# A hybrid decoder block's forget gate: the tokens become the stationary side of its small matmuls, and two transposes go

## The chip, the cores and the metric

The kernel runs on one core of a Trainium2 chip. The metric is the device time of one launch in microseconds (us); lower is better. Three runs of the kernel before took 1178.87, 1178.98 and 1179.95 us (median 1178.98 us).

## The reference, cut to what matters

The layer is one block of a decoder: 256 tokens of width 2048, three attention branches, gates, and an output projection. Everything is float32. One input projection of the normed tokens feeds the branches; eight of its columns are the forget gate's logits `fb`, one for each head of branch B.

```
h = _rmsnorm(x, norm_g[l])
proj = h @ w_in[l]
qa, ka, va, za, qb, kb, vb, zb, fb, qm, zm, gl = _split_cols(proj, IN_WIDTHS)   # fb: 8 columns
...
log_f = jax.nn.log_sigmoid(fb.astype(jnp.float32) + b_forget[l].astype(jnp.float32))
ob = _forgetting_attention(qb, kb, vb, log_f)    # logit[t,s] += sum of log_f over s < j <= t
```

So the gate needs, for each of 256 tokens, 8 sums over 2048 products. It is a very small part of the work: the other columns of `w_in` are 18,432 in number.

## The kernel before, in words

All matmuls on large operands use a split of each float32 value into a high part (the rounded value in the matmul's own 32-bit format, fp32r) and a low part (the rest). A product is then three matmuls: high by high, high tokens by low weights, low tokens by high weights. `hT` holds the high and low parts of the normed tokens, transposed: 128 partitions of the width's rows by 16 tiles `k` by 256 tokens. `mT` is the same for the memory tokens. ScalarE makes the high part of each weight tile (`hi`), VectorE the low part (`lo`), and TensorE runs the three matmuls (`passes`, lines 1220 to 1222) with the tokens as the stationary side and 512 weight columns moving.

The work is cut into units `s` of two weight tiles. A unit is 12 matmuls. Each engine has its own instruction stream in the order in which the code is written, and semaphores tie them together; nothing reorders the streams. In the first 32 units (`body("m", 0, None)`) each engine also runs `beside_first(s)` ahead of or behind unit `s`; this is where tokens and memory tokens are transposed and where the forget gate is computed.

The forget gate's steps before the change, all in the first body:

- TensorE, ahead of unit 12 (lines 1353 to 1362): for each of 16 tiles `k` two matmuls, with the gate's weights as the stationary side (16 columns: the high and low parts of 8 gate columns; then the 8 high ones) and 256 tokens moving. They add up in the PSUM bank `side[0]`, 16 partitions by 256 tokens. The weights lie in a part of the tile `ozT_hi` that is free then (`wf_both`, `wf_hi`).
- VectorE, behind unit 14 (lines 1016 to 1018): a copy of the 16 x 256 result into SBUF (`fbT`, a part of the tile `group`).
- TensorE, ahead of unit 15 (lines 1369 to 1375): two transposes of it, 16 x 128 to 128 x 16, into `side[1]`; then a wait for `dvec_sb`, which has nothing to do with the gate.
- VectorE, behind unit 16 (from line 1021): the sums of the two parts, scaling, bias, and the start of the log sigmoid; ScalarE and VectorE finish it in units 17 to 20, and TensorE forms the running sums over tokens ahead of unit 22 (lines 1380 to 1385).

Ahead of unit 12 TensorE waits for `mT_lo` (the last low part of the memory tokens, VectorE, line 1012) and for the gate's low weights. The tokens' parts `hT` have been there for several units.

Of the kernel before, what the change touches and what calls it, by code (L numbers as in the profile page):

```python
# [37 lines left out]
P = 128  # L38
D = 2048
S = 256  # L40
TT = S // P
KT = D // P
CW = 512
A_HEADS, B_HEADS, M_HEADS, HD, MD = 12, 8, 4, 128, 256
# [68 lines left out]
def hybrid_block(nc, x, mem, norm_g, mem_norm_g, w_in, b_forget, b_gate, rel_bias,  # L113
# [4 lines left out]
    def sb(name, shape, dt=F32):  # L118
        return nc.alloc_sbuf_tensor(name, shape, dt)

    hT = [sb("hT_hi", [P, KT, S], F32R), sb("hT_lo", [P, KT, S], F32R)]
# [8 lines left out]
    def part(at, n):  # L130
        return group[:, at:at + n]
# [22 lines left out]
                                          for at in (8, 12, 16, 20))  # L154
    mem_sb = part(0, 2 * D).rearrange("p (t c) -> p t c", t=TT)
    waste = part(3 * D, D)
    fbT = part(5120, S)[0:2 * B_HEADS]
    cT = part(5120, S)[0:B_HEADS]

    gates = [part(at, 1024).rearrange("p (t c) -> p t c", t=TT) for at in (4096, 1024, 2048)]  # L160
# [7 lines left out]
    ident = cst[:, 0:P]  # L168
# [10 lines left out]
    wf_both = ozT[0][:, 0, 0:KT * 2 * B_HEADS].rearrange("p (k h) -> p k h", k=KT)  # L179
    wf_hi, wf_lo = wf_both[:, :, 0:B_HEADS], wf_both[:, :, B_HEADS:]  # L180
    bf = sb("bf", [P, B_HEADS])
    ls = [sb(f"ls{i}", [P, TT, B_HEADS]) for i in range(8)]
    ccol = sb("ccol", [P, TT, B_HEADS])
# [26 lines left out]
    side = [nc.alloc_psum_tensor(f"side{i}", [P, CW], F32) for i in range(4)]  # L210
# [3 lines left out]
    def x_bank(k):  # L214
# [30 lines left out]
    pre = {n: sem("pre_" + n) for n in (  # L245
        "half rel gains gxT gx sumx0 sumx1 sumx meanx rootx halfx xT x_hi x_lo wf_hi wf_lo dvec dvec_sb dvec_out w_hi w_lo "
        "summ meanm rootm mTp mT_hi mT_lo "
        "fbT fbT_sb fb vb v0 v1 vneg e u ln log1p lf ccol ccol_sb crow_sb crow_out crow_in0 crow_in1 fbias").split()}


    x_v = x.rearrange("b (t p) d -> (b p) t d", p=P)
# [24 lines left out]
    with block as block:  # L276
# [500 lines left out]
        def _(dve):  # L777
# [13 lines left out]
            def chain(name, n, ins):  # L791
                ins.then_inc(pre[name], 1)
                dve.wait_ge(pre[name], n)
# [182 lines left out]
            def beside_first(s):  # L976
# [29 lines left out]
                for r in range(2):  # L1006
                    for j in range(4):
                        if s == 8 + 3 * r + j // 2:
                            dve.wait_ge(pre["mT_hi"], 4 * r + j + 1)
                            for i in range(2):  # L1010
                                k = 8 * r + 2 * j + i
                                o = dve.scalar_tensor_tensor(mT[1][:, k], side[j][:, i * S:(i + 1) * S],
                                                             gm[:, k:k + 1], mT[0][:, k].bitcast(F32),
                                                             ALU.mult, ALU.subtract)
                            o.then_inc(pre["mT_lo"], 1)
                if s == 14:
                    dve.wait_ge(pre["fbT"], 1)
                    dve.tensor_copy(fbT, side[0][0:2 * B_HEADS, 0:S]).then_inc(pre["fbT_sb"], 1)
                if s == 16:

                    dve.wait_ge(pre["fb"], 1)
                    both = side[1][:, 0:TT * 2 * B_HEADS].rearrange("p (t w h) -> p t w h", t=TT, w=2)
                    for t in range(TT):
                        o = dve.scalar_tensor_tensor(ls[1][:, t], both[:, t, 1], rsx[:, t:t + 1], bf[:],
                                                     ALU.mult, ALU.add)
                    chain("vb", 1, o)
                    for t in range(TT):
                        o = dve.scalar_tensor_tensor(ls[0][:, t], both[:, t, 0], rsx[:, t:t + 1], ls[1][:, t],
                                                     ALU.mult, ALU.add)
                    chain("v0", 1, o)  # L1030
                    chain("v1", 1, dve.tensor_scalar(ls[1][:], ls[0][:], -1.0, None, ALU.mult))
                    dve.tensor_tensor(ls[2][:], ls[0][:], ls[1][:], ALU.min).then_inc(pre["vneg"], 1)
# [26 lines left out]
            def body(kind, g, attn, b=None):  # L1059
                u0 = g * BODY_U  # L1060
                for s in range(BODY_U):
# [9 lines left out]
                    if attn is None:  # L1071
                        beside_first(s)
                    else:
                        for t in range(TT):
                            if s == U_Z[t] + 1:
                                silu(attn[1], t)
                        attention(*attn, s)
# [31 lines left out]
            c0 = 4 * GROUPS  # L1109
# [105 lines left out]
        def _(pe):  # L1215
            def passes(s, x_pair, k, j, t, banks, first, last):

                tok = slice(t * P, (t + 1) * P)
                hi, lo = x_pair[0][:, k + j, tok], x_pair[1][:, k + j, tok]
                pe.matmul(banks[t][:], hi, whi[:, s % RING, j], start=first and j == 0, stop=False)  # L1220
                pe.matmul(banks[t][:], hi, wlo[:, s % RING, j], start=False, stop=False)  # L1221
                return pe.matmul(banks[t][:], lo, whi[:, s % RING, j], start=False, stop=last and j == UK - 1)  # L1222
# [86 lines left out]
            def tokens_T(b):  # L1309

                pe.wait_ge(x_in[b], 16)
                for j in range(X_COLS[b] // 256, X_COLS[b + 1] // 256):
                    if j >= 6:
                        pe.wait_ge(pre["x_lo"], 2 * (j - 5))
                    for i in range(2):
                        for t in range(TT):
                            k = 2 * j + i
                            o = pe.transpose(x_bank(k)[:, t * P:t * P + P], x_sb[:, t, k * P:(k + 1) * P], ident)  # L1318
                    o.then_inc(pre["xT"], 1)
# [18 lines left out]
            def beside_first(s):  # L1338
                if s in U_X:
                    tokens_T(U_X.index(s))  # L1340
                if s in (7, 10):
                    r = (7, 10).index(s)
                    pe.wait_ge(mem_in[r], 16)

                    pe.wait_ge(*((pre["mT_lo"], 4) if r else (pre["x_lo"], KT)))
                    for k in range(8 * r, 8 * r + 8):
                        bank = side[(k % 8) // 2]
                        for t in range(TT):
                            c0 = (k % 2) * S + t * P
                            o = pe.transpose(bank[:, c0:c0 + P], mem_sb[:, t, k * P:(k + 1) * P], ident)  # L1350
                        if k % 2:
                            o.then_inc(pre["mTp"], 1)
                if s == 12:

                    pe.wait_ge(pre["mT_lo"], 8)
                    pe.wait_ge(pre["wf_lo"], 1)
                    for k in range(KT):
                        pe.matmul(side[0][0:2 * B_HEADS, 0:S], wf_both[:, k], hT[0][:, k], start=k == 0, stop=False,  # L1358
                                  skip_group_check=True)
                        o = pe.matmul(side[0][0:B_HEADS, 0:S], wf_hi[:, k], hT[1][:, k], start=False,  # L1360
                                      stop=k == KT - 1, skip_group_check=True)
                    o.then_inc(pre["fbT"], 1)
                if s == 13:

                    pe.wait_ge(small_in, 16 * 9)
                    pe.wait_ge(pre["rel"], 1)
                    pe.matmul(side[2][0:A_HEADS, 0:SEG], rel[:], oh[:], start=True, stop=True)\
                      .then_inc(pre["dvec"], 1)
                if s == 15:
                    pe.wait_ge(pre["fbT_sb"], 1)  # L1370
                    for t in range(TT):
                        o = pe.transpose(side[1][:, 2 * t * B_HEADS:2 * (t + 1) * B_HEADS],
                                         fbT[:, t * P:(t + 1) * P], ident[0:2 * B_HEADS, 0:2 * B_HEADS])
                    o.then_inc(pre["fb"], 1)
                    pe.wait_ge(pre["dvec_sb"], 1)
                if s == 22:
                    pe.wait_ge(cst_in, 16)

                    pe.wait_ge(pre["lf"], 1)
                    pe.matmul(side[0][:, 0:B_HEADS], tri[:, 0:P], ls[7][:, 0], start=True, stop=True)  # L1380
                    pe.matmul(side[0][:, B_HEADS:2 * B_HEADS], tri[:, P:S], ls[7][:, 0], start=True, stop=False)
                    pe.matmul(side[0][:, B_HEADS:2 * B_HEADS], tri[:, 0:P], ls[7][:, 1], start=False, stop=True)

                    pe.matmul(side[1][0:B_HEADS, 0:S], ls[7][:, 0], tri, start=True, stop=False)
                    pe.matmul(side[1][0:B_HEADS, P:S], ls[7][:, 1], tri[:, 0:P], start=False, stop=True)\
                      .then_inc(pre["ccol"], 1)
# [25 lines left out]
            c0 = 4 * GROUPS  # L1412
# [20 lines left out]
            for s in range(NCH * CU):  # L1433
# [12 lines left out]
                for t in range(TT):  # L1446
                    for j in range(UK):
                        o = passes(s, mT, UK * (s % CU), j, t, acc[(s // CU) % 2], False, True)
# [45 lines left out]
```

## Time and profile before

| what | value |
|---|---|
| median of three runs | 1178.98 us (1178.87 to 1179.95) |
| profiled execution | 1178.6 us, of which the span of instructions is 1176.8 us |
| TensorE matmuls busy | 1170.0 us, 99% of the span |
| TensorE weight loads busy | 971.9 us, 83% (they lie beside matmuls) |
| VectorE busy | 718.4 us, 61% |
| ScalarE busy | 537.8 us, 46% |
| DMA | 230 GB/s on average |

The span runs from the first to the last instruction of the profiled execution; the execution's own time is 1.8 us longer. A matmul's duration in the trace holds the time until its result is written, and matmuls overlap: with 512 columns moving one is shown as 0.39 us, and the next starts 0.23 us after it. What a matmul costs in a stream is therefore the distance between starts, not its duration. Weight loads (PEld) are rows of their own: "128*16" in a matmul's row is its stationary operand of 128 partitions by 16 columns, and the shape behind it is the moving one.

### The profile page before, as it was taken

The numbers are of one execution on the slowest core, as the hardware profiler recorded it, in microseconds if no ns is written. First come the engines' busy times: TensorE is split into PE (matmuls) and PEld (weight loads), VectorE is DVE, ScalarE is ACT, GpSimd is POOL, SyncE is SP. The second block draws the span as 40 slices with busy tenths as digits, with TensorE's granted clock in tenths as the row PEclk, the third lists the DMA queues.
The fourth block names the chain that finished last, engine by engine and source line by source line (L and its number), as shares of the span: only waits on it lengthen the run. The fifth ranks groups of instructions, "written<-read, shape, count | busy, mean of one in ns | idle before, by whom it ended". The sixth has DMA issues, their size and how long they took to land.

```text
span 1176.8 us, 14683 instructions
## 1 busy us (share of the span) xinstructions
PE 1170.0 (99%) x5332; PEld 971.9 (83%) x5332; DVE 718.4 (61%) x886; ACT 537.8 (46%) x660; POOL 40.6 (3%) x31
## 2 busy tenths in 40 slices
PE   8999999999999999999999999999999999999998
PEld 7888888888888888888888888888888888888887
DVE  5768576576576566567576565665556556555643
ACT  5755445444544544545544444434434443543332
POOL 1100000000010000000000000000000000000000
PEclk9999999999999999999999999999999999999999
DMA  9778678668678587687777786567549547765761
GB/s 312 258 242 309 222 229 295 193 201 312 195 248 282 181 266 260 209 263 225 252 236 237 252 259 216 170 223 254 200 147 302 184 161 225 249 210 204 249 226 38
DMA packets 143848, 270.54 MB, mean 230 GB/s; under 512 B 8833, under 2 KB 29493, under 8 KB 143808
## 3 DMA queue, kind: packets, MB, share of 16 engines
q1 hardware_dynamic: 132032, 253.33, 64.6%
q10 hardware_dynamic: 11488, 16.62, 4.5%
q8 instruction: 25, 0.41, 0.1%
q0 software_dynamic: 288, 0.06, 0.1%
q14 instruction: 15, 0.12, 0.0%
HBM read 248.72 MB, written 23.62 MB: 231 GB/s over the span
## 4 chain that ended last, share of the span: by engine, by line
PE 99%; DMA 0%; DVE 0%; issue 0%
PE acc L1220 32%; PE acc L1221 31%; PE acc L1222 31%; PE side L1270 1%; PE side L1266 0%; PE side L1286 0%; PE acc L1325 0%; PE side L1295 0%; PE side L1297 0%; PE side L1293 0%; PE side L1271 0%; PE side L1350 0%; PE side L1318 0%; DMA cst<-in_consts_dram 0%; PE side L1358 0%; PE side L1360 0%
## 5 line engine op out<-in xcount | busy, mean ns | idle before, releaser
L788 DVE TENSOR_TENSOR w_lo<-w_raw,w_hi 128x1024 fp32r<-128x1024 f32 x407 | 496.1, 1222 | 394.9 <-ACT w_hi L484 394.3
L484 ACT ACTIVATE w_hi<-w_raw 128x1024 fp32r<-128x1024 f32 x407 | 430.1, 1060 | 548.3 <-PE acc L1222 543.5
L1220 PE MATMUL acc<-w_hi,hT_hi 128*128 128x512 f32 x1152 | 450.1, 391 | 0.1
L1222 PE MATMUL acc<-w_hi,hT_lo 128*128 128x512 f32 x1152 | 448.5, 389 | 0.0
L1221 PE MATMUL acc<-w_lo,hT_hi 128*128 128x512 f32 x1152 | 448.4, 389 | 0.0
L1220 PEld LDWEIGHTS acc<-w_hi,hT_hi 128*128 128x128 f32 x1152 | 216.3, 188 | 45.9 <-DVE w_lo L788 1.3
L1222 PEld LDWEIGHTS acc<-w_hi,hT_lo 128*128 128x128 f32 x1152 | 216.2, 188 | 45.2
L1221 PEld LDWEIGHTS acc<-w_lo,hT_hi 128*128 128x128 f32 x1152 | 216.3, 188 | 44.0
L1220 PE MATMUL acc<-w_hi,mT_hi 128*128 128x512 f32 x256 | 100.4, 392 | 0.0
L1222 PE MATMUL acc<-w_hi,mT_lo 128*128 128x512 f32 x256 | 99.7, 389 | 0.0
L1221 PE MATMUL acc<-w_lo,mT_hi 128*128 128x512 f32 x256 | 99.7, 389 | 0.0
L1222 PE MATMUL acc<-w_hi,ozT_lo 128*128 128x512 f32 x224 | 87.2, 389 | 0.0
L1220 PE MATMUL acc<-w_hi,ozT_hi 128*128 128x512 f32 x224 | 87.2, 389 | 0.0
L1221 PE MATMUL acc<-w_lo,ozT_hi 128*128 128x512 f32 x224 | 87.2, 389 | 0.0
L1220 PEld LDWEIGHTS acc<-w_hi,mT_hi 128*128 128x128 f32 x256 | 48.0, 188 | 11.3 <-issue 1.1
L1222 PEld LDWEIGHTS acc<-w_hi,mT_lo 128*128 128x128 f32 x256 | 48.1, 188 | 10.0
L1221 PEld LDWEIGHTS acc<-w_lo,mT_hi 128*128 128x128 f32 x256 | 48.1, 188 | 9.7
L1222 PEld LDWEIGHTS acc<-w_hi,ozT_lo 128*128 128x128 f32 x224 | 42.0, 188 | 8.8
L1220 PEld LDWEIGHTS acc<-w_hi,ozT_hi 128*128 128x128 f32 x224 | 42.0, 188 | 8.7
L1221 PEld LDWEIGHTS acc<-w_lo,ozT_hi 128*128 128x128 f32 x224 | 42.0, 188 | 8.7
L460 POOL TENSOR_TENSOR rs<-ms,half 128x8 f32<-128x8 f32 x10 | 25.6, 2564 | 441.6 <-DVE ms L816 441.6
L575 ACT ACTIVATE group<-acc,rsx 128x512 f32<-128x512 f32 x28 | 19.2, 687 | 20.9 <-PE acc L1222 20.9
(165 smaller groups left out, 542.1 us busy)
## 6 DMA issues: line engine op xcount, KB each, us to landing
w_raw<-in_w_in_dram SPq DMA_DIRECT2D x142, 1024.0 KB, 6.1
w_raw<-in_w_mem_kv_dram SPq DMA_DIRECT2D x16, 1024.0 KB, 7.4
w_raw<-in_w_out_dram SPq DMA_DIRECT2D x16, 1024.0 KB, 5.1
w_raw<-in_w_proj_a_dram SPq DMA_DIRECT2D x12, 1024.0 KB, 5.1
w_raw<-in_w_proj_m_dram SPq DMA_DIRECT2D x8, 1024.0 KB, 5.1
w_raw<-in_w_proj_b_dram SPq DMA_DIRECT2D x8, 1024.0 KB, 5.1
turned_oz<-group SPq DMA_DIRECT2D x40, 128.0 KB, 4.7
group<-turned_oz SPq DMA_DIRECT2D x10, 512.0 KB, 6.0
```

The lines of the kernel that those rows point to most:

```text
L460: pool.tensor_tensor(rs[:], ms[:], half[:], ALU.pow).then_inc(roots, 1)
L484: act.activation(whi[:, s % RING], raw[:, slot, UK * (s % 2):UK * (s % 2) + UK], ACT.Copy)\
L575: act.activation(qn[:, t], acc[w][t][:], ACT.Square, scale=rsx[:, r:r + 1]).then_inc(squares, 1)
L788: dve.tensor_tensor(wlo[:, s % RING], raw[:, (s // 2) % RING, UK * (s % 2):UK * (s % 2) + UK], whi[:, s % RING].bitcast(F32), ALU.subtract ...
L1220: pe.matmul(banks[t][:], hi, whi[:, s % RING, j], start=first and j == 0, stop=False)
L1221: pe.matmul(banks[t][:], hi, wlo[:, s % RING, j], start=False, stop=False)
L1222: return pe.matmul(banks[t][:], lo, whi[:, s % RING, j], start=False, stop=last and j == UK - 1)
L1270: pe.matmul(side[h][:, 0:S], qT[:, 1, h], kT[:, :, h], start=True, stop=True)
```

## The change

The two operands of the gate's matmuls change sides. The tokens' parts, 128 partitions by 128 tokens, are loaded as the stationary side, and the gate's 16 (or 8) weight columns move. The result then lies with the tokens on partitions, 128 x 16 for each half of the tokens, in `side[0]`. Each half of the tokens is its own stationary operand, so there are 64 matmuls in place of 32. The copy of `fbT` on VectorE and the two transposes go, with their two semaphores; VectorE's sums read `side[0]` in place of `side[1]`. The wait for `dvec_sb` stays where it is.

```diff
-    fbT = part(5120, S)[0:2 * B_HEADS]
...
-                if s == 14:
-                    dve.wait_ge(pre["fbT"], 1)
-                    dve.tensor_copy(fbT, side[0][0:2 * B_HEADS, 0:S]).then_inc(pre["fbT_sb"], 1)
                 if s == 16:
 
                     dve.wait_ge(pre["fb"], 1)
-                    both = side[1][:, 0:TT * 2 * B_HEADS].rearrange("p (t w h) -> p t w h", t=TT, w=2)
+                    both = side[0][:, 0:TT * 2 * B_HEADS].rearrange("p (t w h) -> p t w h", t=TT, w=2)
...
                     pe.wait_ge(pre["mT_lo"], 8)
                     pe.wait_ge(pre["wf_lo"], 1)
-                    for k in range(KT):
-                        pe.matmul(side[0][0:2 * B_HEADS, 0:S], wf_both[:, k], hT[0][:, k], start=k == 0, stop=False,
-                                  skip_group_check=True)
-                        o = pe.matmul(side[0][0:B_HEADS, 0:S], wf_hi[:, k], hT[1][:, k], start=False,
-                                      stop=k == KT - 1, skip_group_check=True)
-                    o.then_inc(pre["fbT"], 1)
+                    for t in range(TT):
+                        tok = slice(t * P, (t + 1) * P)
+                        c0 = 2 * t * B_HEADS
+                        for k in range(KT):
+                            pe.matmul(side[0][:, c0:c0 + 2 * B_HEADS], hT[0][:, k, tok], wf_both[:, k],
+                                      start=k == 0, stop=False, skip_group_check=True)
+                            o = pe.matmul(side[0][:, c0:c0 + B_HEADS], hT[1][:, k, tok], wf_hi[:, k], start=False,
+                                          stop=k == KT - 1, skip_group_check=True)
+                    o.then_inc(pre["fb"], 1)
...
                 if s == 15:
-                    pe.wait_ge(pre["fbT_sb"], 1)
-                    for t in range(TT):
-                        o = pe.transpose(side[1][:, 2 * t * B_HEADS:2 * (t + 1) * B_HEADS],
-                                         fbT[:, t * P:(t + 1) * P], ident[0:2 * B_HEADS, 0:2 * B_HEADS])
-                    o.then_inc(pre["fb"], 1)
                     pe.wait_ge(pre["dvec_sb"], 1)
```

TensorE's stream at the head of the gate's matmuls, before. In a row stand the line, what is written from what, and the moving shape's output size; `side` is the PSUM bank, `ozT_hi` holds the gate's weights.

```order
198 L1360 MATMUL side<-hT_lo,ozT_hi 8x256
199 L1358 MATMUL side<-hT_hi,ozT_hi 16x256
200 L1360 MATMUL side<-hT_lo,ozT_hi 8x256
201 L1220 MATMUL acc<-w_hi,mT_hi 128x512 [waits lo_done,pre_mT_lo]
202 L1221 MATMUL acc<-w_lo,mT_hi 128x512
```

The same place now (rows 169 to 232 are the 64 matmuls; lines are those of the changed file):

```order
229 L1357 MATMUL side<-ozT_hi,hT_hi 128x16
230 L1359 MATMUL side<-ozT_hi,hT_lo 128x8
231 L1357 MATMUL side<-ozT_hi,hT_hi 128x16
232 L1359 MATMUL side<-ozT_hi,hT_lo 128x8
233 L1216 MATMUL acc<-w_hi,mT_hi 128x512 [waits lo_done,pre_mT_lo]
234 L1217 MATMUL acc<-w_lo,mT_hi 128x512
```

The block ends ahead of unit 12 as before, with the same waits on the unit's first matmul; there are 32 more rows in it.

TensorE's stream between units 14 and 15, before (`cst` holds the identity, `group` the copy `fbT`):

```order
236 L1221 MATMUL acc<-w_lo,mT_hi 128x512
237 L1222 MATMUL acc<-w_hi,mT_lo 128x512
238 L1372 MATMUL side<-cst,group 128x16 [waits pre_fbT_sb]
239 L1372 MATMUL side<-cst,group 128x16
240 L1220 MATMUL acc<-w_hi,mT_hi 128x512 [waits lo_done,pre_mT_lo,pre_dvec_sb]
```

And now:

```order
268 L1217 MATMUL acc<-w_lo,mT_hi 128x512
269 L1218 MATMUL acc<-w_hi,mT_lo 128x512
270 L1216 MATMUL acc<-w_hi,mT_hi 128x512 [waits lo_done,pre_mT_lo,pre_dvec_sb]
271 L1217 MATMUL acc<-w_lo,mT_hi 128x512
```

The transposes are gone, and unit 15's first matmul keeps its three waits.

## Rows read from the trace of the kernel before

**Rows 1.** The page: busy time, TensorE's granted clock in tenths, and the chain that ended last.

```profile
PE 1170.0 (99%) x5332; PEld 971.9 (83%) x5332; DVE 718.4 (61%) x886; ACT 537.8 (46%) x660; POOL 40.6 (3%) x31
...
PEclk9999999999999999999999999999999999999999
...
PE 99%; DMA 0%; DVE 0%; issue 0%
```

**Rows 2.** Who waited for whom, TensorE: us in total, times, longest.

```profile
PE acc L1325 <- DMA cst<-in_consts_dram: 3.1, 1, 3.1
```

**Rows 3.** Timeline of VectorE beside the gate: with the idle time before, and its releaser.

```profile
47.85 1.65 DVE L1012 SCALAR_TENSOR_TENSOR mT_lo<-side,gm,mT_hi 128x256 fp32r<-128x256 f32 x4
...
53.47 0.41 DVE L1018 COPY group<-side 16x256 f32<-16x256 f32 x1 [0.93 <-PE side L1360]
...
62.87 0.36 DVE L1024 SCALAR_TENSOR_TENSOR ls<-side,rsx,bf 128x8 f32<-128x8 f32 x2 [2.40 <-PE side L1372]
```

**Rows 4.** Timeline of weight loads at the gate's matmuls: start, us, engine, line, operands.

```profile
49.55 0.09 PEld L1358 LDWEIGHTS side<-hT_hi,ozT_hi 128*16 128x16 f32 x1 [0.31 <-DVE mT_lo L1012]
...
53.16 0.19 PEld L1220 LDWEIGHTS acc<-w_hi,mT_hi 128*128 128x128 f32 x1
```

**Rows 5.** Timeline of matmuls at the same place.

```profile
49.56 0.29 PE L1358 MATMUL side<-hT_hi,ozT_hi 128*16 128x256 f32 x1
...
53.27 0.40 PE L1220 MATMUL acc<-w_hi,mT_hi 128*128 128x512 f32 x1
53.51 0.40 PE L1221 MATMUL acc<-w_lo,mT_hi 128*128 128x512 f32 x1
```

**Rows 6.** Timeline of weight loads of the running sums, ahead of unit 22.

```profile
82.05 0.30 PEld L1381 LDWEIGHTS side<-ls,cst 128*128 128x128 f32 x2
82.27 0.30 PEld L1382 LDWEIGHTS side<-ls,cst 128*128 128x128 f32 x2
```

**Rows 7.** Timeline of matmuls of the running sums.

```profile
82.08 0.37 PE L1381 MATMUL side<-ls,cst 128*128 128x8 f32 x2
82.30 0.37 PE L1382 MATMUL side<-ls,cst 128*128 128x8 f32 x2
```

**Rows 8.** Weight loads by line and shape: count, busy us, mean ns, idle before.

```profile
L1220 PEld LDWEIGHTS acc<-w_hi,mT_hi 128*128 128x128 f32 x256 | 48.0, 188 | 11.3 <-issue 1.1 <-DVE w_lo L788 0.4
...
L1350 PEld LDWEIGHTS side<-cst,group 128*128 128x128 f32 x32 | 3.6, 140 | 0.3
...
L1360 PEld LDWEIGHTS side<-hT_lo,ozT_hi 128*8 128x8 f32 x16 | 1.4, 88 | 0.3
```

**Rows 9.** Timeline of matmuls of the memory branch's scores, the first and last of 24.

```profile
113.40 0.28 PE L1266 MATMUL side<-ozT_hi 128*128 128x256 f32 x1
...
116.18 0.28 PE L1266 MATMUL side<-ozT_hi,ozT_lo 128*128 128x256 f32 x1
```

**Rows 10.** Timeline of matmuls: transposes at the start, and later, warm.

```profile
6.27 1.49 PE L1325 MATMUL acc<-cst 128*128 128x128 f32 x6
...
9.48 0.48 PE L1220 MATMUL acc<-w_hi,hT_hi 128*128 128x512 f32 x1
...
32.34 1.91 PE L1350 MATMUL side<-cst,group 128*128 128x128 f32 x16
```

**Rows 11.** Timeline of matmuls at the two transposes, ahead of unit 15.

```profile
62.00 0.39 PE L1221 MATMUL acc<-w_lo,mT_hi 128*128 128x512 f32 x1
62.23 0.39 PE L1222 MATMUL acc<-w_hi,mT_lo 128*128 128x512 f32 x1
62.54 0.29 PE L1372 MATMUL side<-cst,group 16*128 16x16 f32 x2
62.77 0.50 PE L1220 MATMUL acc<-w_hi,mT_hi 128*128 128x512 f32 x1
63.10 0.40 PE L1221 MATMUL acc<-w_lo,mT_hi 128*128 128x512 f32 x1
```

**Rows 12.** Timeline of ScalarE: the read that ends in the signal `dvec_sb`.

```profile
56.98 0.48 ACT L539 ACTIVATE oh<-side 12x384 f32<-12x384 f32 x1 [2.87 <-PE side L1367]
```

More of the change, by code:

```diff
@@ L247, in hybrid_block @@
         "summ meanm rootm mTp mT_hi mT_lo "
-        "fbT fbT_sb fb vb v0 v1 vneg e u ln log1p lf ccol ccol_sb crow_sb crow_out crow_in0 crow_in1 fbias").split()}
+        "fb vb v0 v1 vneg e u ln log1p lf ccol ccol_sb crow_sb crow_out crow_in0 crow_in1 fbias").split()}
     x_v = x.rearrange("b (t p) d -> (b p) t d", p=P)
```

## The prediction

> **What bounds the kernel now.** I read the page first. TensorE's matmuls are busy for 99% of the span, and the chain that ended last is TensorE for 99% too [rows 1]. Then I asked what TensorE waits for: one wait is listed, 3.1 us for the identity at the very start [rows 2]. So TensorE's stream is the time. Whatever lengthens it anywhere behind that first wait lengthens the whole by as much, since no later wait is there to swallow it; and what VectorE saves (61% busy) counts only if TensorE waits for it. The question is thus how long TensorE's stream is at the two places that change, and for that I read the timeline of its matmuls and weight loads there.
>
> **The block of gate matmuls, before.** TensorE waits a little for the last `mT_lo`: VectorE's four instructions start at 47.85 and last 1.65 us, so they end at 49.50 [rows 3], and the first gate load starts at 49.55 [rows 4]. From there 32 pairs of a load and a matmul run until the load of unit 12's first matmul at 53.16 [rows 4]: 3.61 us, 0.113 us a pair. The loads are tiny (16 and 8 columns); each pair streams 256 columns, and that sets the distance. From unit 12's first load to its second matmul it is 53.51 − 53.16 = 0.35 us [rows 4, 5].
>
> **The same block, now.** 64 pairs, each with a load of 128 columns and a matmul of 16 or 8. The trace has no fp32r matmul with so few columns. The nearest row is the running sums ahead of unit 22: 128 x 128 stationary, 8 columns moving, plain float32, which the trace shows as two loads and two matmuls for each instruction. Line 1381's first load starts at 82.05, line 1382's at 82.27: two pairs in 0.22 us [rows 6], and the matmuls agree, 82.08 and 82.30 [rows 7]. That is a pair bound by its load, since 8 columns take next to nothing: a 128-column load is shown as 188 ns and an 8-column one as 88 ns, 100 ns for 120 columns, or 0.107 us for 128 [rows 8]. Those two rows are fp32r, and the running sums' loads last as long (0.30 − 0.11 = 0.19 us [rows 6]), so nothing sets the two formats apart. From above, the scores of the memory branch: fp32r, 128-column loads, 256 columns moving, 24 matmuls from 113.40 to 116.18, 2.78 / 23 = 0.121 us [rows 9]; with less to move it should not be more. From below, the load alone, 0.107 us. The load of the float32 transposes is shown as 140 ns [rows 8], and (140 − 88) / 120 x 128 is 0.055 us; but sixteen of those transposes take 1.91 us, about 0.12 us each [rows 10], so that row does not show loads that follow each other faster, and it is left to a rival. I take 0.111 us for a pair, by the row that is nearest in shape.
>
> The block is then 64 x 0.111 = 7.10 us in place of 3.61: **+3.49 us**. With 0.107 and 0.121 us a pair it is +3.24 and +4.13. The entry does not change: the wait for `mT_lo` ends at the same time, and in both kernels the first load starts only then. The exit does not either: the load of unit 12's first matmul is again followed by that matmul one load later, since in the old kernel the last gate matmul's 256 columns took as long (0.11 us from unit 12's load at 53.16 to its matmul at 53.27 [rows 4, 5]).
>
> **The transposes that go.** Ahead of unit 15, line 1222 starts at 62.23 and unit 15's second matmul at 63.10: 0.87 us [rows 11]. Two ordinary steps are 2 x 0.23 = 0.46 (62.00 to 62.23 is one) [rows 11]. So the two transposes cost 0.41 us, more than half of it because neither their loads nor the load of unit 15's first matmul ran ahead (62.54 is 0.31 behind 62.23, and 63.10 is 0.33 behind 62.77). The wait for `dvec_sb` remains; its signal has been up since about 57.5 us, when ScalarE's read of the matmul ahead of unit 13 ends (56.98 + 0.48 [rows 12]), five us before unit 15, and both move by the same 3.5 us, so I cost it at nothing: **−0.41 us**. If a third wait on that matmul still held its load back, about 0.1 us of this would stay.
>
> **The copy and the sums on VectorE.** The copy is 0.41 us that VectorE no longer spends, plus 0.93 us of waiting for the last gate matmul [rows 3]; VectorE also waited 2.40 us for the transposes ahead of its sums at 62.87 [rows 3]. In the new kernel the gate's result is ready at about 56.7 us, so both waits go. None of this is on the path: the weights' low parts are ahead of TensorE both before and after, since TensorE lists no wait for them [rows 2], and a later TensorE gives them 3 us more. What is late next on VectorE is ScalarE's high parts, which wait for used units and so keep TensorE's pace. Worth 0. The cover that hides it is units 12 to 16 on TensorE, 12 x 0.23 = 2.8 us each. Clearing `side[1]` frees nothing that anyone waits for, worth 0. Nothing on the DMA queues moves.
>
> **The sum**, against the profiled execution: 1176.8 + 3.49 − 0.41 = 1179.9 us of span, 1181.7 us of its own time (1178.6 before). The median of the runs before is 0.4 us above the profiled one, 1178.98, so I forecast 1178.98 + 3.08 = **1182.1 us**, 0.26% slower. With the bounds of the pair (0.107 to 0.121), 0.1 us for the wait and half a us for the scatter of medians, this case covers 1181.3 to 1183.4.
>
> **Rivals.**
>
> *The clock falls in or behind the block.* At the start TensorE runs slow: six transposes in a row take 1.49 us, 0.25 us each, where sixteen later ones of the same shape take 1.91, 0.12 each [rows 10]. That is half the rate, the lower of the two levels (1.2 GHz) by the distance of the rows, although the granted clock is shown as full for the whole span [rows 1]; from the first matmul at 3.1 to unit 0 at 9.48 it stays so [rows 2, 10]. The new block is 7 us in which the array is given 768 moving columns, where a stretch of unit matmuls moves 512 every 0.23 us. If that lets the clock fall and the low stretch lasts as long as the one at the start, 6.4 us at half rate lose 3.2 us: 1185.3. If it is half as long, 1183.7; if it begins in the middle of the block, whose second half would add another 3.5 us, 1188.8. For it: no other stretch of such thin matmuls in this trace is longer than 0.7 us ([rows 6, 7] are its like), so the trace has never tried it. Against it: the loads keep the engine busy without a gap. The Trainium skill, "TensorE: Matmul & The Clock Gate", the section on HAM oscillation, says that a clock once raised falls back when the engine idles between bursts of matmuls, and it does not say whether an array that mostly loads weights counts as idle; by that rule this rival is the result if it does, and no run here shows it yet.
>
> *Pairs closer than the load.* If short matmuls let pairs follow midway between the two load prices, (0.055 + 0.107) / 2 = 0.081 us, the block is 5.18 us, the sum +1.57 − 0.41 = +1.16, and the time 1180.1, no change that can be told. For it speaks only the gap between the 140 and the 188 ns loads [rows 8]; against it stand [rows 6, 7], where 8 columns moved and the pairs still took 0.11. The Trainium skill, the same page, "Back-to-back issue gap", gives 81 ns as the sustained distance of load and matmul pairs with 128 columns moving; by it the time would be the one just given. The trace disagrees: 0.11 us with 8 columns moving [rows 7].
>
> *The other side: two loads in flight.* If fp32r loads of 128 columns really cost 0.055 us, as the transposes' shorter load rows would have it, the block is 64 x 0.056 = 3.58 us, no longer than the old one (−0.03), and with the transposes gone the sum is −0.44: 1178.5, not slower. The point from which it decides is (3.61 + 0.41) / 64 = 0.063 us a pair. Against it: the fp32r loads in this trace are 188 ns throughout [rows 8], not 140, and [rows 6, 7].
>
> **How the numbers follow.** The forecast case 0.73, the clock 0.17, pairs closer than the load 0.06, two loads in flight 0.04. A measurement of this kernel can tell about 0.2% from no change, 2.4 us. The forecast's own range, 1181.3 to 1183.4, is +2.3 to +4.4 us and thus nearly all slower; so is the clock's. Slower 0.87, the same 0.11 (both fast-load cases and the edge of the forecast's), faster 0.02. The range runs from 1180.9 to 1185.3: the forecast's case, the milder half of the clock's, and leaves out the two fast-load cases and a clock that falls early.
>
> **What would show it.** Right: the new lines 1357 and 1359 as 64 matmuls, starts 0.11 us apart, their loads shown as about 188 ns; from the first gate load to unit 12's load 7.1 us; units 14 and 15 with 0.23 us between all matmuls across their border; unit matmuls behind the block 0.39 us long and 0.23 apart. The clock's rival would show in the last: matmuls of 512 columns 0.43 to 0.45 us apart for some us, or gate pairs 0.22 apart. Wrong in size: another distance of the pairs; each 0.01 us is 0.64 us of the result. Wrong altogether: a wait of TensorE later in the kernel that takes up the 3 us, or a new wait ahead of unit 15 or 22.

## The result: slower, by more than twice the forecast

| kernel | median | runs | ratio to before (95% interval) |
|---|---|---|---|
| before | 1178.92 us | 1178.16 to 1179.95 | |
| after | 1186.94 us | 1186.52 to 1188.79 | 1.0070 (1.0058 to 1.0082) |

The change costs 8.0 us where 3.1 us was forecast, and the time lies outside the stated range (1180.9 to 1185.3).

In the changed kernel's page TensorE is still the whole chain. Its busy time and its instructions grew, those of the other engines did not.

```profile
PE 1177.3 (99%) x5362; PEld 978.6 (83%) x5362; DVE 718.3 (61%) x885; ACT 538.1 (45%) x660; POOL 40.6 (3%) x31
...
PEclk9999999999999999999999999999999999999999
...
PE 99%; DMA 1%; SPq 0%; DVE 0%; issue 0%
```

So the loss is to be found on TensorE alone. The timeline of its matmuls over the gate's block (start, duration, line, operands; lines 1357 and 1359 are the gate's two kinds, 1216 to 1218 the passes):

```profile
49.81 0.28 PE L1357 MATMUL side<-ozT_hi,hT_hi 128*128 128x16 f32 x1
...
54.19 0.25 PE L1359 MATMUL side<-ozT_hi,hT_lo 128*128 128x8 f32 x1
54.30 0.26 PE L1357 MATMUL side<-ozT_hi,hT_hi 128*128 128x16 f32 x1
54.41 0.30 PE L1359 MATMUL side<-ozT_hi,hT_lo 128*128 128x8 f32 x1
54.58 0.36 PE L1357 MATMUL side<-ozT_hi,hT_hi 128*128 128x16 f32 x1
54.79 0.35 PE L1359 MATMUL side<-ozT_hi,hT_lo 128*128 128x8 f32 x1
...
59.06 0.35 PE L1359 MATMUL side<-ozT_hi,hT_lo 128*128 128x8 f32 x1
59.27 0.77 PE L1216 MATMUL acc<-w_hi,mT_hi 128*128 128x512 f32 x1
59.84 0.63 PE L1217 MATMUL acc<-w_lo,mT_hi 128*128 128x512 f32 x1
...
64.11 0.63 PE L1218 MATMUL acc<-w_hi,mT_lo 128*128 128x512 f32 x1
64.67 0.82 PE L1366 MATMUL side<-oh,rel 33*12 33x384 f32 x2
65.42 0.50 PE L1216 MATMUL acc<-w_hi,mT_hi 128*128 128x512 f32 x1
65.76 0.40 PE L1217 MATMUL acc<-w_lo,mT_hi 128*128 128x512 f32 x1
```

There are two kernels in this block. Up to 54.41 the pairs follow each other 0.111 us apart, just as the running sums did before [rows 7]. From 54.58 on they are 0.21 us apart, and the twelve 512-column matmuls of unit 12 are 0.43 us apart and shown as 0.63 us long, where in the kernel before they were 0.40 long and 0.24 apart [rows 5] (the first of the twelve, at 59.27, is shown as 0.77 us long and is 0.57 us ahead of the next). At 64.67 it ends. The granted clock says what it is. Below are three stretches of this trace: the columns are length, busy us of PE, PEld, DVE, ACT and POOL with their counts, then the granted clock, the DMA share and GB/s.

```profile
49.80:54.40 4.60, 4.60 (x42) 4.59 (x42) 3.66 (x5) 4.58 (x6) 0.00 (x0) 1.00 0.48 144
54.60:64.60 10.00, 10.00 (x35) 8.45 (x35) 2.26 (x3) 0.00 (x0) 0.70 (x1) 0.50 0.56 188
64.70:1181.00 1116.30, 1116.30 (x5056) 928.22 (x5056) 677.84 (x811) 501.36 (x596) 31.37 (x13) 1.00 0.68 226
```

TensorE's clock falls to its lower level (0.50, 1.2 GHz) in the middle of the block, and is back at the upper one 10 us later. Note PE's busy time: 4.60 of 4.60 us ahead of the fall. A busy share of 100% is no sign that the clock is safe. The page's own 40 slices show a 9 everywhere in the clock's line, and that is luck: a slice is 29.6 us, and the low stretch lies half in the slice that ends at 59.25 us and half in the next, about 5 us in each. In the second profile of this kernel (`e12_after_again`, below) 7 of the 10 us fall into one slice, and the line shows an 8. Here only the mean over the run hints at it, 0.995 in place of 1.000.

The sum of what was lost can be taken from the timelines without the start-up, which differs between executions by up to 3 us (in the traces of this case unit 11's first matmul starts between 46.10 and 49.04 us): from unit 11's first matmul to the last 512-column one it is 1172.85 − 46.78 = 1126.07 us before and 1181.03 − 47.05 = 1133.98 us after, +7.91 us. The rows of both kernels (before first, then after):

```profile
46.78 0.39 PE L1220 MATMUL acc<-w_hi,mT_hi 128*128 128x512 f32 x1
...
1172.85 0.39 PE L1222 MATMUL acc<-w_hi,mT_lo 128*128 128x512 f32 x1
```

```profile
47.05 0.39 PE L1216 MATMUL acc<-w_hi,mT_hi 128*128 128x512 f32 x1
...
1181.03 0.39 PE L1218 MATMUL acc<-w_hi,mT_lo 128*128 128x512 f32 x1
```

This distance is used for all experiments below, and called the body's length. Its parts for the changed kernel: 23 steps from pair to pair from 54.41 to 59.27 take 4.86 us in place of 2.55 (+2.3), and unit 12 to the lone small matmul behind it takes 5.40 us (59.27 to 64.67) in place of 2.89 in a run that kept its clock (below, `e5_wide_moving`), +2.5. That is 4.8 us for the clock; the other 3.1 us are the forecast.

### The profile page after: what moved, and what is told of

Same layout as the page of the kernel before. It is cut to its first block, busy times and chain, and to the rows that moved or that the text cites. A ratio compares the mean times of both kernels' runs of the same rounds, so it can differ in the third digit from the quotient of the medians.

```text
span 1185.0 us, 14742 instructions
## 1 busy us (share of the span) xinstructions
PE 1177.3 (99%) x5362; PEld 978.6 (83%) x5362; DVE 718.3 (61%) x885; ACT 538.1 (45%) x660; POOL 40.6 (3%) x31
## 4 chain that ended last, share of the span: by engine, by line
PE 99%; DMA 1%; SPq 0%; DVE 0%; issue 0%
PE acc L1216 31%; PE acc L1218 31%; PE acc L1217 31%; DMA group<-in_x_dram 1%; PE side L1266 1%; PE side L1262 0%; PE side L1282 0%; PE side L1357 0%; PE side L1359 0%; PE side L1293 0%; PE side L1291 0%; PE side L1289 0%; PE side L1267 0%; PE side L1346 0%; PE side L1314 0%; SPq L308 0%
```

## The experiments

The theory after the trace: (1) a pair costs its load, 0.111 us, and the transposes' 0.41 us come back, +3.1 us in all; (2) the clock falls because TensorE, though busy, mostly loads weights and moves few columns; that costs the other 4.8 us. Rivals: the length of the interruption alone makes the clock fall; the loads themselves do; it was an accident of one execution.

| run | what | median us | ratio to before (95% interval) | body's length, to before |
|---|---|---|---|---|
| after | | 1186.94 | 1.0070 (1.0058 to 1.0082) | +7.91 |
| `e12_after_again` | unchanged | 1187.50 | 1.0072 (1.0055 to 1.0088) | +7.79 |
| `e4_old_twice` | old block, twice | 1182.40 | 1.0024 (1.0015 to 1.0034) | +3.68 |
| `e5_wide_moving` | 128 columns move, gate left out | 1182.13 | 1.0025 (1.0016 to 1.0035) | +3.10 |
| `e11_padded` | the same, gate complete | 1181.97 | 1.0025 (1.0015 to 1.0036) | +3.05 |
| `e2_shadow` | 1 or 2 behind each large one | 1182.18 | 1.0024 (1.0014 to 1.0033) | +3.18 |
| `e1_spread16` | four bursts of 16 | 1183.41 | 1.0033 (1.0020 to 1.0045) | +4.72 |
| `e3_halves` | two bursts of 32 | 1187.34 | 1.0083 (1.0066 to 1.0100) | +7.95 |
| `e9_narrow_loads` | loads of 16 columns, other tokens left out | 1176.46 | 0.9982 (0.9972 to 0.9992) | −2.41 |
| `e6_no_transposes` | before, transposes left out, so no right gate | 1178.18 | 0.9993 (0.9984 to 1.0002) | −0.47 |
| `e10_dvec_beside` | before, a lone matmul moved | 1178.85 | 1.0001 (0.9992 to 1.0010) | 0.00 |

**Is it the length of the interruption?** The old block, issued twice, lasts about as long as the new one would at the upper level.

```diff
-                    for k in range(KT):
+                    for k in list(range(KT)) * 2:
                         pe.matmul(side[0][0:2 * B_HEADS, 0:S], wf_both[:, k], hT[0][:, k], ...
```

> The kernel before with its 32 gate matmuls (16 or 8 columns stationary, 256 moving) issued twice, so that the stretch lasts 7.3 us as in the changed kernel; the second pass overwrites the first with the same sums. Theory (the stretch makes the clock fall since little moves through the array, not since it is long or interrupts the large matmuls): clock stays up, +3.6 us: 1182.6 us. Rival (any long stretch without full-array matmuls lets the clock fall): 0.22 us between the small ones in its last part, 512-column matmuls 0.43 us apart behind it, time 1186 to 1190.

Measured: the clock stays up for the 7.4 us of the block and behind it, and the time is the forecast of the theory within 0.2 us.

```profile
49.50:60.00 10.50, 10.50 (x79) 8.02 (x78) 5.88 (x10) 4.66 (x6) 0.44 (x1) 1.00 0.31 100
```

In the changed kernel the clock fell less than 5 us behind the block's start, so 7.4 us are long enough for the test. The length rival falls. So does the thought that a narrow stationary side (16 of 128 columns) is what lets the clock go: it is narrow here too.

**Is it the loads, or what moves?** Here the loads, their number and their place are the changed kernel's, and 128 columns move.

```diff
-                            pe.matmul(side[0][:, c0:c0 + 2 * B_HEADS], hT[0][:, k, tok], wf_both[:, k], ...
-                            o = pe.matmul(side[0][:, c0:c0 + B_HEADS], hT[1][:, k, tok], wf_hi[:, k], ...
+                            pe.matmul(side[0][:, 0:P], hT[0][:, k, tok], hT[0][:, k, 0:P], ...
+                            o = pe.matmul(side[0][:, 0:P], hT[1][:, k, tok], hT[0][:, k, 0:P], ...
```

> The changed kernel with 128 moving columns (tokens) in place of 16 and 8 in its 64 matmuls; the gate's products are left out, so its result isn't the gate. Same loads, same count, same place. Theory (too few moving columns make the clock fall, the loads set the distance): 128 columns hide under the load of 0.107 us, pairs 0.11 to 0.12 us apart, clock up, time 1182 to 1182.7, faster than the changed kernel although it moves eight times as much. Rival (the loads, 128 columns each in a row, are what the clock does not count, whatever moves): the clock falls as in the changed kernel, 1187 us or more.

Measured: eight to sixteen times the columns, and 4.8 us less than the changed kernel. Its window, and rows from the start of the block (its first matmul, at 48.87, is not shown) and from its end:

```profile
48.80:60.00 11.20, 11.20 (x80) 9.72 (x80) 6.17 (x9) 4.84 (x7) 0.70 (x1) 1.00 0.63 211
```

```profile
49.14 0.27 PE L1357 MATMUL side<-hT_hi 128*128 128x128 f32 x1
49.25 0.28 PE L1359 MATMUL side<-hT_hi,hT_lo 128*128 128x128 f32 x1
...
55.95 0.28 PE L1359 MATMUL side<-hT_hi,hT_lo 128*128 128x128 f32 x1
56.06 0.45 PE L1216 MATMUL acc<-w_hi,mT_hi 128*128 128x512 f32 x1
...
58.95 0.81 PE L1366 MATMUL side<-oh,rel 33*12 33x384 f32 x2
```

Pairs stay 0.111 us apart: 128 moving columns hide under a load of 128. The clock stays up. With equal loads the few moving columns decide, and the loads are not what holds the clock. Widths between 16 and 128 columns were not tried, so how few are too few stays open.

The same with the gate computed in full: each matmul moves the gate's 16 columns and 112 neighbours in the same tile, whose sums land in columns of the bank that nobody reads.

```diff
+                            back = 112 if k >= 8 else 0
+                            c0 = t * S + 112 - back
+                            wide = ozT[0][:, 0, 16 * k - back:16 * k - back + P]
+                            pe.matmul(side[0][:, c0:c0 + P], hT[0][:, k, tok], wide, ...
+                            o = pe.matmul(side[0][:, c0:c0 + P], hT[1][:, k, tok], wide, ...
```

> The changed kernel, computing the gate in full, with each of its 64 matmuls moving 128 columns: the 16 gate columns and 112 neighbours whose results land beside them and are not read. Theory (the moving columns hold the clock; 128 of them hide under a load): pairs 0.11 us apart throughout, clock up, 1182.1 us, 4.8 us faster than the changed kernel with eight times the columns. Rival (the wide run before kept its clock since its operands were the tokens and not the gate's mostly small low parts): clock falls, 1187.

Measured: 1181.97 us, the forecast of 1182.1 within its scatter, and the clock stays up:

```profile
50.00:60.00 10.00, 10.00 (x77) 9.32 (x76) 6.14 (x8) 4.61 (x6) 0.70 (x1) 1.00 0.58 189
```

This also answers the rival that the data matter, since here the gate's own weights move among the rest.

**Is it the one long stretch?** First the 64 matmuls in four bursts of 16 (`if s in (12, 13, 14, 15)`, eight tiles `k` each), then spread singly.

> The changed kernel's 64 small matmuls, 16 ahead of each of units 12, 13, 14 and 15 in place of all 64 ahead of unit 12; all else as changed. Theory (the clock falls because of one long stretch in which TensorE mostly loads weights; each load-and-matmul pair itself costs 0.111 us): each burst of 16 takes 1.8 us with 2.7 us of 512-column matmuls between, the clock stays at its upper level, all pairs 0.111 us apart, time 1182.1 us (+3.1 on before). Rival (the clock falls for another reason, as the sum of small matmuls or the exchange of operands itself): 512-column matmuls 0.43 us apart are seen again, time 1185 to 1187.

Measured: 1183.41 us, between the two. The trace (of an execution of 1182.97 us) shows a short fall, once, behind the second burst:

```profile
55.45 0.25 PE L1360 MATMUL side<-ozT_hi,hT_lo 128*128 128x8 f32 x1
55.63 0.81 PE L1368 MATMUL side<-oh,rel 33*12 33x384 f32 x2
56.38 0.70 PE L1216 MATMUL acc<-w_hi,mT_hi 128*128 128x512 f32 x1
56.88 0.63 PE L1217 MATMUL acc<-w_lo,mT_hi 128*128 128x512 f32 x1
...
59.87 0.43 PE L1218 MATMUL acc<-w_hi,mT_lo 128*128 128x512 f32 x1
60.13 0.39 PE L1216 MATMUL acc<-w_hi,mT_hi 128*128 128x512 f32 x1
```

3.5 us at half rate are 1.7 us, and 4.72 − 3.1 = 1.6 is what it lost. The expectation that a burst of 16 keeps the clock was wrong for this burst and right for the three others. Nor does the fall seem to come each time: of the six executions five have a mean granted clock of 0.998 or 0.999 and took 1182.97 to 1183.81 us, and one has 1.000 and took 1182.19 us, the time with the clock held. So a burst of 16 is a borderline case here. The second burst differs in having the lone small matmul of the relative-position bias right behind it; whether that tips it was not tried.

The single spread puts one or two small matmuls behind each large one (a list of the 64, taken from inside `passes`).

> The changed kernel's 64 small matmuls put one or two at a time behind each 512-column matmul of units 12 to 15 (16 a unit: 1, 1 and 2 behind the three passes). Theory (a pair costs its load, since the next load can start only once the matmul before has taken over its weights): the first small matmul's load hides under the 512 columns, but the next large load is then exposed, so each still costs 0.11 us: 1182.1 us. Rival (loads that hide under a large matmul are free): two thirds of the 64 loads vanish, block 64 x 0.03 to 0.05 us, time 1176.5 to 1178.5, which would beat both kernels. The clock stays up under both.

Measured: clock at 1.00 over the whole stretch, 1182.18 us. The hope that a load hidden under 512 columns is free fell. The stretch's window, the loads, then the matmuls:

```profile
49.30:68.60 19.30, 19.30 (x116) 16.40 (x116) 7.56 (x12) 7.21 (x9) 0.70 (x1) 1.00 0.42 138
```

```profile
50.60 0.19 PEld L1220 LDWEIGHTS side<-ozT_hi,hT_hi 128*128 128x128 f32 x1
50.83 0.19 PEld L1234 LDWEIGHTS acc<-w_lo,mT_hi 128*128 128x128 f32 x1
```

```profile
50.60 0.39 PE L1232 MATMUL acc<-w_hi,mT_hi 128*128 128x512 f32 x1
50.83 0.17 PE L1220 MATMUL side<-ozT_hi,hT_hi 128*128 128x16 f32 x1
50.85 0.48 PE L1234 MATMUL acc<-w_lo,mT_hi 128*128 128x512 f32 x1
51.17 0.17 PE L1223 MATMUL side<-ozT_hi,hT_lo 128*128 128x8 f32 x1
```

The small matmul's load (50.60) does hide under the large matmul that starts with it. But the next large load starts only when the small matmul does (50.83), and 16 columns hide next to nothing of it: 50.60 to 51.17 is 0.57 us for one large, one small and one large, 0.11 more than two large ones (0.46).

**Two bursts of 32**, ahead of unit 12 and unit 14:

> The changed kernel's small matmuls in two bursts of 32: the first half of the tokens ahead of unit 12, the second ahead of unit 14, with 5.4 us of 512-column matmuls between. Theory: the pairs cost the same 3.1 us in all; each burst of 3.6 us may let the clock fall as the bursts of 16 did once, and since a burst is half as long, less of it and of what follows is slow than in the changed kernel: 1182.1 to 1185.5 us, the excess over 1182.1 equal to half the time at the low level. Rival (a burst of half the length keeps the clock): 1182.1.

Measured: 1187.34 us, no better than one block, and worse than either theory foresaw. The clock falls twice: once 1 us behind the end of the first burst (it ends at 53.50), once in the last four pairs of the second:

```profile
54.70:57.90 3.20, 3.20 (x9) 2.24 (x7) 2.24 (x3) 0.00 (x0) 0.70 (x1) 0.52 0.52 131
58.10:64.70 6.60, 6.60 (x42) 5.44 (x43) 1.23 (x1) 2.60 (x3) 0.00 (x0) 0.99 0.58 208
64.80:70.80 6.00, 6.00 (x17) 4.90 (x17) 2.20 (x7) 0.22 (x1) 0.00 (x0) 0.50 0.27 81
```

About 9.7 us at the lower level again, now mostly paid by large matmuls. Half of that, 4.85 us, is the excess in the body (7.95 − 3.1), as expected; what was wrong is that half a burst would mean a shorter time at the low level. Here halving the thin stretch did not halve its price.

**Was it an accident?** The changed kernel profiled again:

> The changed kernel unchanged, on another chip or at another time, profiled again. Theory (its own block makes the clock fall each time, at a point that can shift): the same pattern, 0.22 us between pairs in a last part of the block, 512-column matmuls 0.43 us apart behind it, back at 0.23 us within unit 12 or 13; time 1186.5 to 1189. Rival (the fall was an accident of the first profile): clock up throughout, 1182.

Measured: the same pattern, the fall at 56.6 in a block that starts later (51.78), and 9.9 us at the lower level; 1187.50 us. No accident: all seven executions of the changed kernel have a mean granted clock of 0.994 to 0.997, and none of the kernel before has less than 0.998. The page's clock line, then the matmuls:

```profile
PEclk9989999999999999999999999999999999999999
```

```profile
56.49 0.28 PE L1357 MATMUL side<-ozT_hi,hT_hi 128*128 128x16 f32 x1
56.63 0.36 PE L1359 MATMUL side<-ozT_hi,hT_lo 128*128 128x8 f32 x1
56.85 0.36 PE L1357 MATMUL side<-ozT_hi,hT_hi 128*128 128x16 f32 x1
```

**What sets the 0.111 us?** The same 64 matmuls with 16 tokens stationary in place of 128 (`tok = slice(t * P, t * P + 16)`, output rows 0 to 16).

> The changed kernel's 64 gate matmuls with 16 tokens stationary in place of 128 (gate wrong for the other tokens: left out), still 16 and 8 columns moving. Theory (a pair costs its load): loads of 16 columns, pairs 0.03 to 0.07 us apart, the block 2 to 4.5 us in place of 9.5 and the time 1177 to 1180 unless the clock falls in it. Rival (0.11 us is a floor of every pair, whatever its load): pairs stay 0.11 us apart and the clock falls, 1187.

Measured: 0.026 us a pair, the whole block 1.7 us.

```profile
49.49 0.17 PE L1359 MATMUL side<-ozT_hi,hT_lo 128*16 128x8 f32 x1
49.52 0.17 PE L1357 MATMUL side<-ozT_hi,hT_hi 128*16 128x16 f32 x1
...
51.11 0.17 PE L1359 MATMUL side<-ozT_hi,hT_lo 128*16 128x8 f32 x1
51.13 0.48 PE L1216 MATMUL acc<-w_hi,mT_hi 128*128 128x512 f32 x1
```

So 0.111 us is the load of 128 columns, and no floor of every pair. The pairs were closer than the lower end that was expected (0.03), and the time, 1176.46 us, lies below the 1177 of the expectation for that reason. The clock stayed up, in a stretch of 1.7 us.

**What do the transposes cost?** The kernel before, with the copy and the transposes left out:

> The kernel before without the copy on VectorE and the two transposes; VectorE's sums read the untransposed bank, so the gate's values are not the gate's. It takes the changed kernel's gain alone. Theory: TensorE saves the 0.41 us of the prediction (0.23 us between all matmuls from unit 14 to unit 15), time 1178.5 to 1178.6. Rival (the wait for dvec_sb ahead of unit 15, a third wait on that matmul, still holds its load back): 0.1 to 0.2 us of it stays, 1178.8. The medians can hardly tell, the trace can.

Measured: from unit 14's to unit 15's first matmul 2.72 us (60.23 to 62.95) where it was 3.04 (59.73 to 62.77). The step behind it is 0.23 us where it was 0.33, which makes 0.42 us of the 0.47 us less in the body. The median moves by 0.6 us, with an interval that holds no change. The third wait costs nothing: unit 15's first matmul follows at 0.22 us.

```profile
60.23 0.39 PE L1217 MATMUL acc<-w_hi,mT_hi 128*128 128x512 f32 x1
...
62.73 0.39 PE L1219 MATMUL acc<-w_hi,mT_lo 128*128 128x512 f32 x1
62.95 0.39 PE L1217 MATMUL acc<-w_hi,mT_hi 128*128 128x512 f32 x1
63.18 0.39 PE L1218 MATMUL acc<-w_lo,mT_hi 128*128 128x512 f32 x1
```

**A version better than both?** One try to shorten the kernel before: the bias's lone matmul moved next to the gate's block, to share a break.

> The kernel before with the one matmul of the relative-position bias (line 1367, 33 x 12 stationary) moved from ahead of unit 13 to right behind the gate matmuls ahead of unit 12. Theory (what such a lone small matmul costs between units is mostly the break: its own load and the next large load do not run ahead, 0.32 and 0.34 us where 0.23 are usual): one of the two breaks is shared, 0.2 to 0.35 us saved, 1178.7 us, visible in the trace alone. Rival (the cost is the matmul's own): no change in the distance from unit 11 to unit 14.

Measured: nothing, 0.00 us in the body. The lone matmul now starts 0.21 us behind the last gate one (54.08 to 54.29) and the next large one 0.74 us later, as before. The rival held: its cost is its own. No kernel here that computes the gate beats the one before; `e11_padded` and `e2_shadow` are the best with the tokens stationary, 3.2 and 3.1 us behind it in the median, which does not tell them apart.

## Why the prediction was wrong, point by point

- **TensorE's stream is the time, and nothing later swallows a loss.** Right: +7.91 us in the body, +8.0 in the median.
- **64 pairs at 0.111 us, +3.49 us.** Right wherever the clock stayed up: 0.111 in the first 41 steps of the changed kernel and in all of `e5_wide_moving`. The row of the running sums, plain float32 with 8 columns, was the right stand-in, and `e9_narrow_loads` shows that the load is what it measures.
- **The transposes give back 0.41 us.** Right: 0.47 in the body of `e6_no_transposes`. The split of it was misread: the two steps whose loads did not run ahead are 0.31 and 0.33 us where 0.23 is usual, 0.18 us together, less than half of the 0.41; the two transposes' own step (62.54 to 62.77) is the other 0.23.
- **VectorE's side is worth nothing.** Right as far as shown: TensorE waits nowhere new around the block. The two waits that the changed kernel's list adds, 0.6 us for `x` and 0.3 us for a `w_lo`, lie in the start-up, ahead of 13 us.
- **The sum, +3.08 us.** It is the measured +3.05 to +3.10 of the two wide runs. (The upper bound that the prediction adds up comes to 1183.3, not 1183.4; nothing hangs on it.) What was forecast is what this change costs with the clock held.
- **The clock.** This is the step that failed. The sum has no term for it: the forecast case takes TensorE's clock to stay at its upper level, on the argument that "the loads keep the engine busy without a gap", and gives the fall 0.17. What the runs showed in its place is a fall in the block in every execution of the changed kernel, worth 4.8 us. `e5_wide_moving` against the changed kernel shows that loads do not hold the clock. As a rival the prediction had the mechanism, its place and its signs right (in the block, 0.22 us between pairs, 0.43 between large matmuls). Its price was off: it took the low stretch at the start of one execution as the measure, 6.4 us long; measured were 10 us, of which 4.6 us lay in the block, from about two thirds of it on. The variant of a fall in mid-block (1188.8 us) was 1.9 us too high, and the range left out just that variant. The start is no steady measure either: the same six transposes that took 1.49 us before [rows 10] took 1.03 us in the changed kernel's trace, with the next six at 0.82, so the low stretch there was over about 4 us behind the first matmul.
- **The two rivals with cheaper pairs** (0.081 and 0.055 us) fell: in a row of thin pairs with loads of 128 columns none came closer than 0.111 us in any run. (Only a small matmul right behind a 512-column one, under which its load is hidden, starts closer, and the next one pays for it.) The Trainium skill, "TensorE: Matmul & The Clock Gate", gives 81 ns as a sustained distance with 128 columns moving ("Back-to-back issue gap"); `e5_wide_moving` and `e11_padded` show 111 ns for fp32r. The measurement decides.

The Trainium skill's rule on the clock (same page, "HAM oscillation"), that it falls when the engine idles between bursts, is to be read with this trace: here it fell with matmuls shown as busy 4.60 of 4.60 us ahead of the fall.

## What to carry to other kernels

Choosing the stationary side is a choice of who pays: a 128-column load takes 0.111 us, while the 256 moving columns that do the same work take 0.113 us; swapping put the same 256 tokens through two loads, and doubled the block. Where a matmul has few moving columns, it costs its load, and here up to 128 moving columns were free beside a load of 128: move them, because 128 also held the clock. Ahead of a thin stretch ask not whether TensorE is busy but what it moves, and price a fall of the clock with the large matmuls that follow it, since in these runs half of the loss or more fell on them.

## What the hardware showed that I had not expected

- The clock fell 4.6 to 4.8 us behind the start of the block in both profiles of the changed kernel, while the matmul rows left no gap, and stayed low for about 10 us, of which 5.4 us were 512-column matmuls.
- Splitting the thin stretch in two made two falls (`e3_halves`); four bursts of 16 made one in the profiled execution (`e1_spread16`); single small matmuls between large ones made none (`e2_shadow`).
- Loads of 16 columns with 16 or 8 moving ones follow each other at 0.026 us.
- At the start of every trace the first transposes (two groups of four, 1.11 or 1.12 us each) are at half the later rate, although the granted clock of that stretch reads 1.00; in the middle of the run it reads 0.50 where the rows are slow. How long the slow start lasts differs between executions: six transposes right behind take 1.49 us in the kernel before [rows 10], 1.03 in the changed kernel and 0.88 in `e3_halves`. That the start is slow because of the clock is read from the distance of the rows alone.
